# Gate-row additions behind the gathered copies, other ring slots for a layer's first units, and the down products in another half order, in a two-layer hybrid block with a mixture of experts

## The reference

```python
def block(x, mod, lp, ctx=None):
    sh1, sc1, g1, sh2, sc2, g2 = jnp.split(mod, N_MOD, axis=-1)
    h = rmsnorm(x, lp['norm1_g']) * (1 + sc1) + sh1
    y, new = token_mixing(h, lp, ctx)
    x = x + g1 * y
    h = rmsnorm(x, lp['norm2_g']) * (1 + sc2) + sh2
    x = x + g2 * ec_moe(h, lp['w_router'], lp['w_gate'], lp['w_up'], lp['w_down'])
    return x, new

def ec_moe(h, w_router, w_gate, w_up, w_down):
    cap = CAPACITY_FACTOR * n // N_EXPERTS          # 16 prompt tokens, 32 sample tokens
    aff = jax.nn.softmax(jnp.einsum('bnd,de->ben', h, w_router), axis=1)
    vals, idx = lax.top_k(aff, cap)                 # each expert picks its tokens
    xg = jax.vmap(lambda hb, ib: hb[ib])(h, idx)
    a = jnp.einsum('becd,edf->becf', xg, w_gate)
    u = jnp.einsum('becd,edf->becf', xg, w_up)
    o = jnp.einsum('becf,efd->becd', jax.nn.silu(a) * u, w_down) * vals[..., None]
    return  # o added back to the tokens at idx
```

## Time and profile before

| | before |
|---|---|
| median of 3 runs | 1867.62 us (1863.84 to 1871.46) |
| profiled execution | 1864.66 us |
| its span, first to last instruction | 1862.9 us |
| mean granted clock of PE | 0.986 of 2.4 GHz |
| PE busy | 1737.4 us (93%) |
| DVE, ACT, POOL busy | 494.6, 293.7, 115.3 us |
| moved by DMA | 531.77 MB, mean 285 GB/s |

### The profile page before, as it was taken

The page is one execution under the profiler, slowest core; times in us unless marked ns, Lnnn a source line. Parts: engine busy times, 40 slices in busy tenths (PEclk is TensorE's granted clock), DMA queues, the critical chain, the costliest instruction groups (busy, mean ns, idle before and its releaser), DMA issues.

```text
span 1862.9 us, 19013 instructions
## 1 busy us (share of the span) xinstructions
PE 1737.4 (93%) x7336; PEld 808.5 (43%) x7336; DVE 494.6 (27%) x1132; ACT 293.7 (16%) x736; POOL 115.3 (6%) x156
## 2 busy tenths in 40 slices
PE   6998999999899999898899989999998999988987
PEld 3455555554434333242245555555543343323322
DVE  1345333212312111121124344332132121201211
ACT  2233222100201010010022333221011010100000
POOL 1151000000000000000012400000000000000000
PEclk9998999999999999999999989999998999999999
DMA  9452111542899999999992701117328999999997
GB/s 383 187 221 80 68 68 68 228 172 91 340 430 430 430 432 429 433 429 431 385 409 92 277 24 68 68 68 304 147 84 360 429 431 431 431 431 430 430 430 337
DMA packets 48528, 531.77 MB, mean 285 GB/s; under 512 B 5776, under 2 KB 6832, under 8 KB 9808
## 3 DMA queue, kind: packets, MB, share of 16 engines
q1 hardware_dynamic: 45776, 524.45, 67.8%
q0 software_dynamic: 1536, 5.87, 0.9%
q10 hardware_dynamic: 1152, 0.56, 0.1%
HBM read 528.73 MB, written 2.13 MB: 285 GB/s over the span
## 4 chain that ended last, share of the span: by engine, by line
PE 75%; DMA 20%; DVE 2%; ACT 2%; issue 1%; SPq 0%; ACTq 0%; DVEq 0%
PE bank L1883 23%; DMA ring<-in_w_moe 18%; PE bank L1529 13%; PE bank L1548 7%; PE bank L1594 6%; PE bank L1753 5%; PE bank L1924 3%; PE bank L1630 2%; PE bank L1479 2%; PE bank L1818 2%; PE bank L1695 2%; DMA ring<-in_w_mix 1%; PE bank L1557 1%; PE bank L1668 1%; PE bank L1572 1%; PE bank L1517 1%
## 5 line engine op out<-in xcount | busy, mean ns | idle before, releaser
L1529 PE MATMUL bank<-hT,ring 128*128 128x384 f32 x768 | 259.8, 492 | 0.0
L1883 PE MATMUL bank<-M,hT 128*64 128x512 f32 x1024 | 232.4, 604 | 29.3 <-DMA M<-in_w_moe 22.4
L1883 PE MATMUL bank<-ring,hT 128*64 128x512 f32 x1024 | 226.3, 594 | 14.1 <-DMA ring<-in_w_moe 14.1
L1529 PEld LDWEIGHTS bank<-hT,ring 128*128 128x128 f32 x768 | 143.5, 190 | 105.0 <-issue 11.6
L1883 PEld LDWEIGHTS bank<-M,hT 128*64 128x64 f32 x1024 | 74.5, 139 | 184.4 <-issue 158.8
L1883 PEld LDWEIGHTS bank<-ring,hT 128*64 128x64 f32 x1024 | 73.0, 137 | 164.8 <-issue 147.1
L1548 PE MATMUL bank<-M,ring 128*128 128x384 f32 x384 | 134.2, 492 | 11.1 <-ACT M L757 11.1
L1883 PE MATMUL bank<-M 128*64 128x512 f32 x512 | 113.9, 594 | 8.5 <-DMA M<-in_w_moe 4.6
L1594 PE MATMUL bank<-ring,hT 128*128 128x512 f32 (+1 forms) x288 | 117.4, 567 | 1.5 <-DVE hT L1037 1.5
L1883 PE MATMUL bank<-ring,M 128*64 128x512 f32 x512 | 113.8, 595 | 5.3 <-DMA ring<-in_w_moe 4.6
L939 ACT ACTIVATE hT<-bank 128x512 f32<-128x512 f32 x32 | 19.1, 597 | 627.3 <-PE bank L1883 627.3
(11 more groups left out here) (224 smaller groups left out, 1491.4 us busy)
## 6 DMA issues: line engine op xcount, KB each, us to landing
M<-in_w_moe SPq DMA_DIRECT2D x96, 2048.0 KB, 30.2
ring<-in_w_moe SPq DMA_DIRECT2D x96, 2048.0 KB, 30.2
ring<-in_w_mix SPq DMA_DIRECT2D x110, 1024.0 KB, 7.0
ring<-in_w_mix SPq DMA_DIRECT2D x4, 576.0 KB, 3.7
M<-in_counts POOLq DMA_DIRECT2D x2, 768.0 KB, 13.0
out<-x SPq DMA_DIRECT2D x6, 256.0 KB, 2.6
x<-in_x_sample SPq DMA_DIRECT2D x1, 1024.0 KB, 8.6
M<-in_b_mod POOLq DMA_DIRECT2D x2, 512.0 KB, 5.8
```

What stands on the lines that cost most here:

```text
L1529: ins = mm(ps[:, 0:TOK], w[:, q, (j % 4) * P:(j % 4 + 1) * P], hT[:, 4 * h + q, :], start=(h == 0 and q == 0), stop=(h == 1 and q == 3))
L1883: ins = mm(bank[b][64 * e:64 * e + 64, :], lhs(e, 4 * h + q), w[:, q, :], start=(h == 0 and q == 0), stop=(h == 1 and q == 3))
```

## The change

- `plan_units` lists the first twelve units in another order, which gives them other slots. A new list `ISSUE` keeps the order in which they are issued: mod 0 (two halves), mod 2 (two), segment 0's first half, mod 1 (two), mod 3 (two), segment 1's first half, segment 0's second, segment 1's second. Mod 0 now goes to slots 0 and 1, mod 2 to 2 and 3, segment 0 to 4, mod 1 to 5 and 7, mod 3 to 6 and 0.
- The row of mod 2 in layer 1 is copied by ACT, behind its squares of x.
- The two additions to `g2slot` stand behind DVE's first gathered copies.
- In each pair the order of the transfers of the down products is down 0 first half, down 1 first half, down 0 second half, down 1 second half, in DRAM, on SP and on PE. PE's order in a pair becomes: gate 0, up 0, gate 1, turn 0, turn of the chosen values, up 1, down 0 first half, turn 1, (gather), down 1 first half, down 0 second half, down 1 second half, combines; in the layer's last pair `combine(0)` stands before down 1's second half.
- ACT copies the chosen values between its two copies of hidden values.

```diff
 def plan_units():
     units = []
-    for i in (0, 2):
-        units += [("mod", i, 0), ("mod", i, 1)]
-    units += [("seg", 0, 0)]
-    for i in (1, 3):
-        units += [("mod", i, 0), ("mod", i, 1)]
-    units += [("seg", 1, 0), ("seg", 0, 1), ("seg", 1, 1)]
+    units += [("mod", 1, 1), ("mod", 0, 0), ("mod", 0, 1), ("mod", 2, 0), ("mod", 2, 1), ("seg", 0, 0), ("mod", 1, 0),
+              ("mod", 3, 0), ("seg", 1, 1), ("mod", 3, 1), ("seg", 1, 0), ("seg", 0, 1)]
...
+ISSUE = [1, 2, 3, 4, 5, 6, 0, 7, 9, 10, 11, 8] + list(range(12, NU))
...
             def wait_pair(l, gr, c, j):
-                g, h = j // 2, j % 2
+                g, h = (j // 2, j % 2) if j < 8 else (4 + j % 2, j // 2 - 4)
...
-                for n, u in enumerate(UNITS):
+                for n in ISSUE:
+                    u = UNITS[n]
...
                     mod_row(l, 0)
                     for kb in BACK[1::2]:
                         h_raw(l, kb)
-                    mod_row(l, 2)
+                mod_row(l, 2)
...
                 normalise(0)
-                if l > 0:
-                    mod_row(l, 2)
                 first_variance(2)
...
                 chosen(0, (0,))
-                for i in (10, 11):
-                    ps = wait_full(dve, l, ("modb", i, 0))
...
                 dve.wait_ge(xpad_zero, l + 1)
                 gathered(0)
+                for i in (10, 11):
+                    ps = wait_full(dve, l, ("modb", i, 0))
+                    c = (i - 10) * 512
+                    V.tensor_tensor(g2slot[:, c:c + 512], ps[:, :], g2slot[:, c:c + 512], ALU.add)\
+                        .then_inc(bank_read[turn(l, ("modb", i, 0))[0]], 1)
...
+                    def project(g, b, h, lhs):
+                        if h == 0:
+                            begin_pair(b, PROJECT[b])
+                        j = 12 * c + (2 * g + h if g < 4 else 4 + 2 * h + g)
+                        s = DOUBLES[j % ND]
+                        pe.wait_ge(landed[s], 16 * (l * LANDS[s] + LANDED[s] + gr * (24 // ND) + j // ND + 1))
+                        for q in range(4):
+                            for e in range(2):
+                                w = expert_slot(s + e)
+                                ins = mm(bank[b][64 * e:64 * e + 64, :], lhs(e, 4 * h + q), w[:, q, :],
+                                         start=(h == 0 and q == 0), stop=(h == 1 and q == 3))
+                        ins.then_inc(first_half_used if h == 0 else bank_full[b], 1)
...
+                    project_up(0, BANK_G[0])
+                    project_up(1, BANK_U[0])
+                    project_up(2, BANK_G[1])
+                    turn_product(0)
+                    turn_values()
+                    project_up(3, BANK_U[1])
+                    begin_pair(BANK_T, 1)
+                    project_down(0, 0)
+                    turn_product(1)
+                    if more:
+                        gather_sample(gr + 1, range(4))
+                        gather_prompt(gr + 1)
+                    project_down(1, 0)
+                    begin_pair(BANK_T, 2)
+                    project_down(0, 1)
                     if last:
                         combine(0)
-                    project_down(1)
+                    project_down(1, 1)
                     if not last:
                         combine(0)
                     combine(1)
...
-    return out.reshape(L, NP, 12, P, 2 * UNIT)
+    out = out.reshape(L, NP, 12, P, 2 * UNIT)
+    return np.concatenate([out[:, :, 0:8], out[:, :, 8:12:2], out[:, :, 9:12:2]], axis=2)
```

More of the change, by code:

```diff
@@ L943, in group_step @@
                                 .then_inc(bank_read[BANK_T], 1)
-                        act.wait_ge(bank_full[BANK_Y], in_pair(l, BANK_Y, gr, c, 0) + 1)
-                        F(selT, bank[BANK_Y][:, 0:TOK], ACT.Copy).then_inc(bank_read[BANK_Y], 1)
+                            if h == 0:
+                                act.wait_ge(bank_full[BANK_Y], in_pair(l, BANK_Y, gr, c, 0) + 1)
+                                F(selT, bank[BANK_Y][:, 0:TOK], ACT.Copy).then_inc(bank_read[BANK_Y], 1)
                         if c and more:
@@ L1381, in _ @@
                 chosen(0, (0,))
-                for i in (10, 11):
-                    ps = wait_full(dve, l, ("modb", i, 0))
-                    c = (i - 10) * 512
-                    V.tensor_tensor(g2slot[:, c:c + 512], ps[:, :], g2slot[:, c:c + 512], ALU.add)\
-                        .then_inc(bank_read[turn(l, ("modb", i, 0))[0]], 1)
                 k = 1
@@ L1872, in begin_pair @@
                         pe.wait_ge(bank_read[b], in_pair(l, b, gr, c, k))
-                    def project(g, b, lhs):
-                        begin_pair(b, PROJECT[b])
-                        for h in range(2):
[L1877 to L1896, removed]
+                    def project(g, b, h, lhs):
+                        if h == 0:
+                            begin_pair(b, PROJECT[b])
[8 more added lines that the diff above has]
+                        ins.then_inc(first_half_used if h == 0 else bank_full[b], 1)
@@ L1897, in pair_step, with project_up, project_down, turn_product @@
+                    def project_up(g, b):
+                        for h in range(2):
+                            project(g, b, h, lambda e, kb: xcur[:, kb, 2 * c + e, :])
+                    def project_down(n, h):
+                        project(4 + n, BANK_D[n], h, lambda e, kb: hidT[:, kb, 64 * e:64 * e + 64])
+                    def turn_product(h):
                         begin_pair(BANK_T, h)
@@ L1902, in pair_step, with turn_values @@
                         ins.then_inc(bank_full[BANK_T], 1)
[L1904 to L1915, removed]
+                    def turn_values():
+                        begin_pair(BANK_Y, 0)
+                        pe.wait_ge(vsel_ready, l * 2 * NP + 2 * (2 * gr + c) + 2)
+                        for t in range(T):
+                            ins = turn_over(bank[BANK_Y][:, t * P:(t + 1) * P], vsel[:, t, :], ident)
+                        ins.then_inc(bank_full[BANK_Y], 1)
                     def combine(n):
@@ L1925, in combine @@
                                start=True, stop=True).then_inc(bank_full[b], 1)
-                    project_down(0)
+                    if c == 0:
+                        pe.wait_ge(xcur_ready, (l * NG + gr + 1) * 12)
+                        for b in range(4):
+                            begin_pair(b, 1)
+                    project_up(0, BANK_G[0])
[13 more added lines that the diff above has]
+                    project_down(0, 1)
                     if last:
                         combine(0)
-                    project_down(1)
+                    project_down(1, 1)
                     if not last:
```

## The result

| | before | after |
|---|---|---|
| median | 1868.7 us (6 runs, 1862.6 to 1871.46) | 1851.93 us (6 runs, 1850.41 to 1854.03) |
| ratio | | 0.9922, 95% interval 0.9905 to 0.994 |
| profiled execution, span | 1864.66, 1862.9 | 1852.09, 1850.3 |
| mean granted clock | 0.986 | 0.992 |

Faster by 0.8%. The prediction said 1857.7 (1851 to 1864.5). The profiles differ by 12.6 us, the medians by 16.8. In 54 other runs of the kernel before, timed on three later occasions, the mean is 1865.2, so some 3 us of the 16.8 are scatter of the first six runs.

The account below looks back on a forecast made before the run. Expert transfers were taken to bound each layer's experts, so only PE time at their start and tail counts. Terms -4.9 - 5.9 + 1.35 - 1.0 + 0.5 = -9.95 us from 1867.62 gave 1857.7, range 1851 to 1864.5.

Parts of the forecast that it names:

- The first expert product 3.25 us earlier in each layer: Start of each layer's experts: with the additions behind the gathered copies, PE's first expert product starts 3.25 us earlier.
- The clock stays up there, 1.65 and 2.65 us: Start of the experts: without PE's idle time its clock stays at 2.4 GHz; with the earlier start, -4.9 and -5.9 us.
- The tail, +1.35 in each layer: End of each layer's experts: the first down product needs the third down transfer, so the last combine comes 1.35 us later.
- The middle is worth 0: Middle of the experts: the new order removes PE waits of 1 to 3 us per pair, covered by the transfers: 0.
- The boundary, -2.35: Between the layers: new slots and ACT's row copy bring layer 1's first segment product earlier, -2.35 us alone, -1.0 net.
- POOL's loads, +0.5: Layer 0's start: POOL's loads start 2.4 us earlier and take bandwidth from the weights, +0.5 us (0 to 0.8).
- (b): Rival: more gained, as the median run loses more at both expert starts and tails cost nothing; -13, 1854.6; chance 0.16.
- (a): Rival: the clock still falls at the start of the experts, only 2 x 3.25 gained there; -5.65, 1862.0; chance 0.14.
- (c): Rival: gathered copies don't free PE, or DVE gets its banks late; boundary and part of start remain; -3, 1864.6; chance 0.11.
- (d): Rival: slower, PE's clock falls in the experts' last pairs, where PE waits in short pieces; up to 1887; chance 0.04.
- more than 11 us: Sign of a wrong prediction: layer 1's first segment starts more than 11 us behind the last combine.

Follow-up runs that it names:

- e1: Kernel before with only the gate-row additions moved behind the gathered copies: 1853.36 us, ratio 0.9931.
- e2: Kernel before with three extra PE products, result never read, behind the gate rows ahead of the first expert product: 1858.41 us, ratio 0.996.
- e7: Kernel after with the gate-row additions put back ahead of the gathered copies: 1861.23 us, ratio 0.9983 to the kernel before.
- e5: Kernel after, but each layer's last pair keeps the old half order of the down products: 1850.13 us, ratio 0.9919 to the kernel before.
- e6: Kernel after with four extra PE products at six places in the middle of the experts, 23 us of PE work: 1854.37 us, ratio 0.9948 to before.
- e9: Kernel before with the new half order and PE order in all pairs but each layer's last: 1863.3 us, ratio 0.9989.
- e12: Kernel before with the extra PE products of e2 and e8 and no other edit: 1851.75 us, ratio 0.9922.
- e10: Kernel before with the new slots alone, the row of mod 2 in layer 1 still copied by DVE: 1861.62 us, ratio 0.9977.
- e3: Kernel before with only the new half order of the down products and PE's new order in a pair: 1864.39 us, ratio 0.9987.
- e4: Kernel before with only the new slots for first units and the row of mod 2 copied by ACT: 1860.73 us, ratio 0.997.
- e8: Kernel of e5 with extra PE products ahead of the last turn of the latent keys and ahead of the gather: 1842.84 us, ratio 0.988 to before.
- e11: Kernel of e8 without the three products at the latent keys, keeping the one ahead of the gather: 1848.21 us, ratio 0.99 to before.

## Why the prediction was right, and where it was off

The sign was right and the time fell inside the range, though near its lower end and outside the forecast's own 1855 to 1861: it came 5.8 us below the forecast of 1857.7. Some 2.4 of these are the starting point, since 1867.62, the median of three runs, lies that much above the mean of the 54. The rest is a gain larger than the 10 us forecast. By its own steps, on the profiles (12.6 us):

- *The first expert product 3.25 us earlier in each layer*: G is 2.84 and 4.79 less. The first 24 products of layer 0's gather took 0.34 us longer than before (4.54 against 4.20 us), those of layer 1's 1.55 us less (2.92 against 4.47), by the clock they met. That 1.55 is luck of this execution and no effect of the change; it is the largest part of what the profiles gained beyond the forecast. The term is right without it: 7.14 to 3.95 us behind the last gather block, 3.19.
- *The clock stays up there, 1.65 and 2.65 us* (by the prediction's own rows 1.73 and 2.76, so that its -4.9 should be -5.0): shown by e1, and by e2 on its own; 1.7 and 2.8 by E of before against e1. e7 takes it back. The Trainium skill (TensorE: Matmul & The Clock Gate, HAM oscillation) names an idle gap as the cause; e2 agrees, whose E falls by 1.9 and 2.6 us once the gap is filled. That the effect varies from run to run stands in another section of the Trainium skill (TensorE: Matmul & The Clock Gate, What's actually happening) than the one that the prediction names; the twelve cold starts agree, with 5.35 to 6.47 us for the same work.
- *The tail, +1.35 in each layer*: 1.45 in layer 0 and 1.69 in layer 1 (after against e1), 1.5 by e5. E changed by -0.28 and -1.10, where clock and tail together were forecast at -0.3 and -1.3.
- *The middle is worth 0*: shown by E in e6 and by e9.
- *The boundary, -2.35*: -3.08. The size was off because I kept PE's columns and transposes at the pace of the kernel before, whose clock was low there; the segment product came 2.6 us behind the third normalisation, not 3.24. e12 confirms it: with before's slots and the full clock it is also 2.60 (936.85 to 939.45). e10 parts the 3.1 into 2.6 for the slots and 0.5 for the row. What I did not see at all is that the half order already frees the first slot earlier: e3 has 2.6 of the 3.1 us without any new slots. So the half order and the slots gain the same 2.6 us, once. Together they cost 3.1 us of tails (1.45 + 1.69) and give 3.1 at the boundary, which is nothing; all that the whole change gains by the marks comes from the additions (e1) and from the clock that the gather met.
- *POOL's loads, +0.5*: they start 2.9 us earlier, and the first product of segment 1 comes at 40.81 instead of 40.49, although the one before it started 0.44 us earlier (36.48 and 36.92). So 0.76 us were lost there, but at 184 us the two kernels are level again: the same product starts at 184.37 and 184.35. Whether the loads are the cause is not shown. The wait for the unit is there in seven of the eight kernels with the new slots (0.6 to 1.25 us), but also in e9 (1.26 us), whose slots and loads are those of before. The term did not reach the end.

```profile
23.53 0.74 POOL L621 DMA_DIRECT2D rows<-in_rows  x1 [7.82 <-DMA ring<-in_w_mix]
...
40.81 3.70 PE L1591 MATMUL bank<-ring,hT 128*128 128x512 f32 x8 [0.69 <-DMA ring<-in_w_mix]
```

The remaining 0.5 us lie in layer 1's mixing part, in a stretch of changing clock. Between the profiles' 12.6 and the medians' 16.8 stands scatter. It goes with the clock: over 54 runs of the kernel before, time and mean granted clock have a correlation of -0.88, 1.4 us for each 0.001. Where in the kernel it arises is open. The standard deviation is 1.2 us after and 1.9 to 2.9 on the three occasions before, and an execution before can lose more or less at each start of the experts (5.4 and 6.4 us for a transfer in the same profile). But e1 and e2 don't lose there either, and scatter by 2.8 and 2.6 us (five runs each); the low clock also comes and goes at the gather, at the layers' boundary and in attention.

The medians also give single parts more than their profiles do: e2 7.9 against 4.5, e4 5.6 against 3.1, and e1 13.0 against 9.9 by G and E. In all three the profiled execution was the slowest of its kernel. The sign of each of these parts is sure, its size only to some 3 us.

Of the rivals, (b) was nearest by the number (1854.6). Its first reason, that the median run loses more at the two starts than the profiled one, is open: e2's medians speak for it, but the longest cold start of all these profiles (6.47 us) leaves only 1.2 us more to lose there than this profile lost (5.35 and 6.37). Its second, that the tails cost nothing, is wrong. (a), (c) and (d) did not occur.

One sign was set wrongly. The first segment product of layer 1 starts 11.17 us behind the last combine (929.09 to 940.26), and "more than 11 us" was to show that the prediction was wrong. Its own working gives 11.85 (933.6 to 945.45), and before it was 14.24, so the limit should have lain above its own 11.85.

## What to carry to other kernels

Where a full transfer queue sets the end, look for what starts it and for the work behind its last item: 1.4 us of DVE work per layer and its wait, ahead of the wrong copies, cost about 13 us here (e1), and PE waits saved in 14 of 16 pairs gave nothing (e9). Price an idle PE twice, once for the gap and once for the clock of what follows; a few products whose result nobody reads can be the cheapest edit (e8, e12). Time each part of a change alone: two parts that close the same gap do not add up (e3 and e10), and the last item of a loop may want another order than the rest (e5).

## What the runs showed of the hardware that I had not expected

- Extra PE work made the kernel faster: 7 extra products per layer in the kernel before gave 13 us (e12), with the mean clock at 0.996 over its runs instead of 0.986.
- A low clock during the gather did not carry over into the expert products (e1: 0.51, then 1.00), while 3.4 us without work brought it down behind a gather at full clock (e9: 1.00, then 0.66 over the first 5 us).
- A stretch of 10 us at the start of attention (166 to 176) ran at 1.2 GHz in part in every profile but those of e8 and e12, where it is at 1.00. Taking that away was worth some 2 us in layer 0 by the trace (420.09 against 422.24) and 5.4 us in both layers by the medians (e8 against e11), though PE is busy for only 7.3 of these 10 us in the kernel before.
